# Two more places for expert weights, other waits ahead of their loads, and a part of the state chain moved, in two transformer blocks with 32 experts

## The reference

```python
h = h + mixed @ w_out[l]                       # mixed = [retention, recurrence]
xn = rms_norm_2(h, norm2_gain)
# each token goes to 2 of 32 experts, D = 1024, D_EXPERT = 512
def expert_block(args):
    xblk, e = args
    hdn = jax.nn.silu(xblk @ w_gate[e]) * (xblk @ w_up[e])
    return hdn @ w_down[e]
# recurrence, step by step
sa = einsum('bhvk,bhk->bhv', state, a_t)
state = state * w_t + sa[..., None] * b_t + v_t[..., None] * k_t
```

## Time and profile before

| | us |
|---|---|
| timed runs | 1047.58, 1049.62, 1049.64 |
| median | 1049.62 |
| the profiled execution, its own time | 1047.48 |
| its span (first to last instruction) | 1045.7 |
| TensorE busy | 900.0 |
| VectorE busy | 436.9 |
| ScalarE busy | 318.1 |

### The profile page before, as it was taken

How to read it: one execution, slowest core, us unless ns; L and a number is a source line. 1 busy time by engine, 2 the same in 40 slices (tenths; PEclk the granted TensorE clock), 3 DMA queues, 4 the chain that set the end, 5 groups by cost and what they waited for, 6 DMA issues and landing times.

```text
span 1045.7 us, 17915 instructions
## 1 busy us (share of the span) xinstructions
PE 900.0 (86%) x7768; PEld 642.5 (61%) x7768; DVE 436.9 (42%) x553; ACT 318.1 (30%) x410; POOL 17.5 (2%) x34
## 2 busy tenths in 40 slices
PE   5999999999999998999999997776868677677854
PEld 5999988999999878999988732221313122121311
DVE  4577777666656437996676510000101010010101
ACT  4457674554444327644443400000000000000002
POOL 1300000000000000000000000000000000000000
PEclk9999999999999999999999999998989888998999
DMA  9994334555654544353019999999999999999994
GB/s 338 269 325 147 133 111 162 161 162 171 204 190 161 201 155 163 129 205 115 3 56 387 420 398 422 422 421 420 421 421 423 421 422 422 421 422 423 422 421 193
DMA packets 84439, 294.97 MB, mean 282 GB/s; under 512 B 5903, under 2 KB 35231, under 8 KB 59664
## 3 DMA queue, kind: packets, MB, share of 16 engines
q1 hardware_dynamic: 79280, 284.18, 69.8%
q10 hardware_dynamic: 3552, 6.08, 1.6%
q0 software_dynamic: 1536, 3.68, 1.3%
HBM read 290.77 MB, written 4.10 MB: 282 GB/s over the span
## 4 chain that ended last, share of the span: by engine, by line
PE 55%; DMA 31%; SPq 5%; DVE 5%; issue 2%; ACT 1%; DVEq 0%; ACTq 0%
PE psum L986 13%; DMA arena<-in_w_down 13%; PE psum L987 13%; PE psum L988 13%; DMA arena<-in_w_up 12%; DMA arena<-in_w_gate 5%; SPq L837 5%; PE psum L1572 4%; PE psum L1315 3%; PE psum L961 2%; PE psum L1592 2%; DVE ring_rounded L2055 1%; PE psum L953 1%; PE psum L1061 1%; DVE arena L2103 1%
## 5 line engine op out<-in xcount | busy, mean ns | idle before, releaser
L1572 PE MATMUL psum<-arena,featL 128*32 128x512 f32 x1024 | 172.1, 657 | 63.6 <-DMA arena<-in_w_up 48.6
L2055 DVE TENSOR_TENSOR ring_rounded<-arena,hi_rounded 128x2048 fp32r<-128x2048 f32 x77 | 176.0, 2290 | 94.7 <-ACT hi_rounded L1677 93.8
L1677 ACT ACTIVATE hi_rounded<-arena 128x2048 fp32r<-128x2048 f32 x77 | 146.7, 1912 | 157.5 <-PE psum L988 52.4
L986 PE MATMUL psum<-hi_rounded,featT_rounded 128*128 128x256 f32 (+1 forms) x560 | 165.2, 295 | 4.7 <-DVE featL_rounded L2071 3.9
L987 PE MATMUL psum<-ring_rounded,featT_rounded 128*128 128x256 f32 (+1 forms) x560 | 162.6, 290 | 0.0
L988 PE MATMUL psum<-hi_rounded,featL_rounded 128*128 128x256 f32 (+1 forms) x560 | 162.5, 290 | 0.0
L1572 PEld LDWEIGHTS psum<-arena,featL 128*32 128x32 f32 x1024 | 38.7, 118 | 184.9 <-DMA arena<-in_w_up 86.3
L1592 PE MATMUL psum<-arena,featT 128*32 128x512 f32 x488 | 91.7, 673 | 40.9 <-DMA arena<-in_w_down 36.0
L986 PEld LDWEIGHTS psum<-hi_rounded,featT_rounded 128*128 128x128 f32 x560 | 108.0, 193 | 8.3 <-DVE ring_rounded L2055 4.2
L987 PEld LDWEIGHTS psum<-ring_rounded,featT_rounded 128*128 128x128 f32 x560 | 108.1, 193 | 1.2
L988 PEld LDWEIGHTS psum<-hi_rounded,featL_rounded 128*128 128x128 f32 x560 | 108.0, 193 | 1.3
(11 more groups left out here) (295 smaller groups left out, 1138.9 us busy)
## 6 DMA issues: line engine op xcount, KB each, us to landing
arena<-in_w_gate SPq DMA_DIRECT2D x75, 1024.0 KB, 26.2
arena<-in_w_up SPq DMA_DIRECT2D x75, 1024.0 KB, 26.4
arena<-in_w_down SPq DMA_DIRECT2D x62, 1024.0 KB, 26.9
arena<-in_w_in SPq DMA_DIRECT2D x14, 2048.0 KB, 8.9
arena<-in_w_down SPq DMA_DIRECT2D x5, 2048.0 KB, 7.7
arena<-in_w_out SPq DMA_DIRECT2D x3, 2048.0 KB, 8.6
arena<-in_w_in SPq DMA_DIRECT2D x4, 1024.0 KB, 9.6
t_copies<-arena ACTq DMA_DIRECT2D x1, 2048.0 KB, 8.0
```

What stands on the lines that cost most here:

```text
L986: mm(o, lhs[0], rhs[0], start=start, stop=False, skip_group_check=True)
L1572: ins = mm(psum[32 * j:32 * j + 32, MB[4 + m], :], xg[:, 4 * half + k, 32 * j:32 * j + 32], quad[place(q, j)][j][:, 512 * k:512 * k + 512] ...
L1677: fn(high, view, ACT.Copy).then_inc(hi_ready, 1)
L2055: tt(low, view, high.bitcast(F32), ALU.subtract).then_inc(lo_ready, 1)
```

## The change

- **Places.** `SPLIT` adds a place 6 for j = 2 (half in `featL`, half in `featT`, where the space of the one-hot rows is laid out anew) and for j = 3 (1024 floats in `rows`, where the final gain goes later, 512 in `featT`, 512 in a new tile `late`). `ONCE` becomes (2, 1, 2, 2), and `FIRST` lists for each j in which place its first loads go. A split piece comes in two or three DMAs. `held` finds its columns.
- **Waits.** `place_free` names a place and the pieces in it; the waits ahead are others, and in another order. To make this possible the mask `mle` moves out of the stretch of `cst` that a piece overwrites, the inverse's P2T to another slot, and the states S from `arena` into free halves of `xn`.
- **Final gain.** GpSimd loads it behind its four small products and behind eight read pieces.
- **Chain.** The keys of state 0 go ahead of WT on TensorE. `root` goes ahead of the copies of Q and gn on ScalarE, and `ret_scale(1)` ahead of TT on VectorE.

The diff, cut to its core:

```diff
-LE = layout(("G", 256), ("Gw", 256), ("GT", 256), ("sg", 512), ("h", 512))
+LE = layout(("G", 256), ("Gw", 256), ("sg", 512), ("h", 512), ("GT", 256), ("gap", 256))
...
-             ("reset", T), ("gap2", 64), ("wina", 64),
-             ("mAdT", 64), ("mAd", 64), ("m16T", 64), ("m32T", 64), ("mlt", 64), ("mle", 64), ("id64", 64),
+             ("mle", 64), ("reset", T), ("gap2", 64), ("wina", 64),
+             ("mAdT", 64), ("mAd", 64), ("m16T", 64), ("m32T", 64), ("mlt", 64), ("id64", 64),
...
-        AdT, Ad, o16T, o32T, X, P2, P2T = (piece(M0 + 1024 * n, NT, 8, CH) for n in (0, 1, 2, 3, 12, 13, 4))
+        AdT, Ad, o16T, o32T, X, P2, P2T = (piece(M0 + 1024 * n, NT, 8, CH) for n in (0, 1, 2, 3, 12, 13, 11))
...
-        S = piece(LM["RT"][0], NCH, 4, 64)
+        S = [xn[:, c // 2, 512 + 256 * (c % 2):768 + 256 * (c % 2)].rearrange("p (i v) -> p i v", v=64) for c in range(NCH)]
...
+        late = sb("late", [P, 512])
+        SPLIT = {2: (featL[:, 4:8, :].rearrange("p a b -> p (a b)"), spent[:, LE["sg"][0]:LE["h"][1]]),
+                 3: (final_gain, spent[:, LE["GT"][0]:LE["gap"][1]], late[:])}
...
-        ONCE = (2, 1, 1, 1)
+        ONCE = (2, 1, 2, 2)
+        FIRST = [(*PLACES, NQ, NQ + 1)] * 2 + [(PLACES[0], NQ + 2, *PLACES[1:], NQ)] * 2
...
-                    at = quad_place(r, pair, q, j)
-                    nc.sync.dma_start(quad[at][j], w[:, j, 2048 * half:2048 * half + 2048]).then_inc(quad_in[at][j], 16)
+                    at, lo = quad_place(r, pair, q, j), 2048 * half
+                    for part in (quad[at][j],) if at < NQ + 2 else SPLIT[j]:
+                        nc.sync.dma_start(part, w[:, j, lo:lo + part.shape[1]]).then_inc(quad_in[at][j], 16)
+                        lo += part.shape[1]
...
+                    wait_filled(sp, "ro", NT - 1)
+                    place_free(2, 0, 1)
+                    wait_filled(sp, "mat", "Arb", 1)
+                    place_free(3, 3)
+                    sp.wait_ge(mixed_ready, 1)
+                    place_free(2, 2)
+                    wait_filled(sp, "gn", NT - 1)
+                    place_free(NQ, 0, 1)
+                    wait_filled(sp, "mat", "Ark", 1)
+                    place_free(3, 2)
                     sp.wait_ge(mixed_ready, NT)
-                    load_quad(0, 0, 0, pieces=(1, 2, 3))
-                    wait_emptied(sp, "mat", "Ark", 1)
-                    load_quad(0, 0, NQ, pieces=(0, 1))
-                    for key, pieces in RELEASED:
-                        wait_filled(sp, *key)
-                        for q, k in pieces:
-                            load_quad(0, 0, q, pieces=(k,))
+                    wait_filled(sp, "U", NCH - 1, 1)
+                    place_free(2, 3)
+                    wait_filled(sp, "Y", 1, 1)
+                    place_free(3, 0, 1)
                     sp.wait_ge(mixed_ready, 2 * NT)
-                    load_quad(0, 0, NQ, pieces=(2,))
-                    load_quad(0, 0, 2, pieces=(2,))
+                    place_free(NQ, 2)
+                    place_free(1, 2)
                     wait_filled(sp, "wo2", 0, 1)
-                    load_quad(0, 0, 2, pieces=range(2))
-                    load_quad(0, 0, 3, pieces=(3,))
+                    place_free(1, 0, 1)
+                    place_free(0, 3)
                     wait_filled(sp, "wo2", 1, 0)
-                    load_quad(0, 0, 2, pieces=(3,))
-                    load_quad(0, 0, 3, pieces=(0,))
+                    place_free(1, 3)
+                    place_free(0, 0)
                     wait_filled(sp, "wo2", 1, 1)
-                    load_quad(0, 0, 3, pieces=(1, 2))
+                    place_free(NQ + 2, 2, 3)
+                    place_free(0, 1, 2)
...
-            wait_filled(pool, "logit", NT - 1)
-            nc.gpsimd.dma_start(final_gain, A["final_gain"].to_broadcast([P, D])).then_inc(gain_in, 16)
...
+            pool.wait_ge(pieces_read, 8)
+            nc.gpsimd.dma_start(final_gain, A["final_gain"].to_broadcast([P, D])).then_inc(gain_in, 16)
...
+            st0 = state_keys(0)
             banks = [begin("WT", c).rearrange("p (t i q) -> p t i q", t=NT, i=4) for c in range(2)]
...
-            st0 = state_keys(0)
             u_inner(0)
...
                 if name == "Z2":
                     high_moved("mT", 0, 0)
+                    root(48, RET_H, RET_D, 1)
...
-                    root(48, RET_H, RET_D, 1)
...
                 if name == "Z2":
                     low_moved("mT", 0, 0)
-                if name == "TT":
                     ret_scale(1)
```

## The result

The changed kernel is slower, by less than half a per cent. Its median is 1050.78 us (1048.24 to 1059.39, 19 runs) against 1047.59 (1045.03 to 1052.51, 19 runs) for the kernel before, 3.2 us more. Forecast were 3.3 us less.

The account below looks back on a forecast made before the run. The prediction took the unbroken expert-weight DMA stream (about 421.7 GB/s) as the bound. Queue -3.5, split pieces +0.4 and chain -0.2 gave -3.3 us, from the median 1049.62 to 1046.3; range 1042.5 to 1049.8.

Parts of the forecast that it names:

- the model of the queue's holes: Expert-weight queue: 23 places close the 601 to 605 hole, unbroken run from 576.5, end at 1025.3, 3.5 us less.
- The final gain: Its 0.52 MB load moves from ahead of the idle hole into the unbroken run, costing 1.25 us.
- the moved steps: TensorE chain up to 574.38: keys of state 0 ahead of WT gain 0.2 us; the moved scaling and root, zero.
- the split pieces: Two pieces in DMAs with 4 and 2 KB rows, 2.1 MB in all: taken as 0.4 us more.
- The bound from above: For the split pieces: 2.1 MB at w_out_2's 376 GB/s instead of 422, 0.6 us more.
- The estimate of 1.2: For the split pieces: at the skill's 341 GB/s for a single 1 MB DMA, 1.2 us lost.
- rival 2: Expert traffic in 499.6 to 504.6 and 533.7 to 545.8 delays TensorE's instruction fetches; slower 0.06, most gain eaten 0.14.
- The price of one fetch: In rival 2: 1.0 us per delayed fetch; slower only with five or six delays, or fewer longer ones.
- The argument against it: Against rival 2: in 545 to 555 DMA already ran at 379 GB/s with TensorE busy 9.2 of 10 us.
- what the early loads bring: Ahead of the unbroken run: each MiB landed before it is worth 2.49 us.
- Rival 3: Early places come late in SyncE's order, so only the added places count: 1.6 us gained, 1048.0; chance 0.14.
- Rival 1: Full gain or more: the 557.2 stall shrinks by 1.0 us, splitting is free, -4.7, 1044.9; 0.66 together with the forecast.

Follow-up runs that it names:

- late_no_split: late_all without the two added places: 21 places, no piece in parts, the final gain's load where the change puts it; 1050.43 us, ratio 1.0021.
- chain_only: The kernel before with only the three moved chain steps, its first expert loads also waiting for U of chunk 0; 1047.84 us, ratio 1.0005.
- rows_4k: The kernel before with the two pieces issued at 586.84 us cut into four DMAs with rows of 4 KB; 1047.65 us, ratio 0.9997.
- late_all: The changed kernel with its six early pieces issued only when TensorE has U of chunk 0; 1047.0 us, ratio 0.9992.
- late_parts: The changed kernel, its six early pieces and piece 3's `late` part waiting for U of chunk 0, its `rows` part for VectorE's last U copy; 1043.81 us, 0.9967.
- old_chain: The changed kernel with the keys of state 0, the square root and the scaling back in their old order; 1049.83 us, ratio 1.0021.
- traffic_at_ro: The kernel before with four unused 1 MiB copies, all issued when the retention output is filled (near 497 us); ratio 1.0046.
- traffic_on_before: The kernel before with four unused 1 MiB copies, issued at Arb, the first scaled retention half and gn; 1056.83 us, ratio 1.0085.

## Why the prediction was wrong, point by point

**Right: the model of the queue's holes.** 23 places close the hole of 601 to 605 (416 GB/s), the queue is empty just before 577 (183 GB/s in 574 to 577; it was forecast empty up to 576.5, and the sum of wo2 came 1.6 us later than in before), and the last stretch runs at 421. The start-up time, too, fits. The final gain was rightly taken from the idle hole into the bill: 1.25 us forecast, and late_no_split shows 1.8 in all.

**Right: the moved steps cost nothing.** chain_only, 1.0005. VectorE's last step, of two instructions, stood at 539.89 and 540.82 in before and was forecast there; it came at 537.81 and 538.79, which counted from the `ro` copy is 0.2 us later, behind TensorE's pause of 0.30 us for the first late fetch. In chain_only it is 0.7 us or more earlier than in before. The 0.2 us gained can't be seen at this resolution.

**Wrong in size: the split pieces.** Taken at 0.4 us, with bounds 0 and 0.6, from the rate of w_out_2. The row length was costed rightly (0.3 us in rows_4k). What failed is the assumption that a piece in parts differs from a whole one in nothing but its rows: 587 to 600 at 370 instead of 419 GB/s is 1.5 us, and the unequal end of the DMA engines is 0.8. Together 2.3 in place of 0.4, which leaves 1.2 of the 3.5 us that the queue should have gained; 0.8 were measured, and 0.4 isn't placed. The bound from above was the error: a nearest row with shorter rows in an unloaded queue is no bound for five DMAs into four tiles in a full one. The estimate of 1.2 that I worked out from the Trainium skill ("DMA: Bandwidth & Descriptors", section Bandwidth) was nearer than my bound, though its reason, the size of one DMA, isn't what the runs show: rows_4k has DMAs of 512 KB at 408 to 412 GB/s.

**Wrong: the step that decided, the price of the early traffic.** The prediction has this mechanism as its rival 2, a fetch of TensorE's instructions that expert traffic holds back, and gives "slower" 0.06. Three steps of it failed.
1. The price of one fetch. I took the difference of two stalls, 1.0 us, and asked for five or six of them. Two fetches in a row under a queue at 348 to 418 GB/s, 3.3 and 6.2 us late, cost a stall of 3.05 us. Priced one by one, a second late fetch behind the first wasn't in the rival's sum.
2. The argument against it. "545 to 555 has DMA at 379 GB/s too and TensorE busy 9.2 of 10 us" is true and proves little. The one fetch of TensorE's that starts in that stretch, at 550.63, is 3.1 us late; TensorE went on, so it must have had instructions left. The next, at 556.86, is 3.4 us late, and that is the stall of 2.05 us at 557.2. A busy TensorE was no sign of a fetch in time.
3. The consequence. A stall under which TensorE is idle isn't paid once: the granted clock was 0.50 for the next 10 us. Against late_all the chain lost 4.0 us. The stall is 3.05 of it; the half clock on the work behind it should be the rest (by difference; no run has the one without the other), and the stall of 1.77 us at 556.7 of late_all, which after doesn't have, gives some of it back.

**Wrong: what the early loads bring.** I counted each early MiB as 2.49 us. But up to 577 the places that are free are few, and the queue catches up. In after it stands idle in 546 to 552 (3 GB/s) and again in 574 to 577; late_all uses this very time for the pieces that it has not loaded early. Its window ahead of the sum of wo2:

```profile
565.00:570.00 5.00, 5.00 (x42) 4.82 (x41) 1.70 (x4) 1.20 (x2) 0.00 (x0) 1.00 1.01 419
```

By 574 to 577 it, too, falls to 341 GB/s: it has caught up. With the six pieces issued together behind 543 the queue takes 456.3 us, with them early 456.0. The prediction's own sum had this in it: its twelve pieces landed by 573.6 "and the queue is empty for 2.9 us". The slack of the queue ahead of 574 had to be set against the early loads, and it would have shown that they could be left out. What brings the gain is the number of places and what fills them, which late_parts gets without early traffic.

**Rival 3** (late places, 1048.0) is, by late_all, nearly that: 1047.0, ratio 0.9992, and harmless. **Rival 1**'s step came true, the stall at 557 is gone in after, where DMA is idle, but at the price of a larger one.

**What stays open.** Why the stretch with parts into `featL`, `featT`, `rows` and `late` runs at 317 to 348 GB/s for 7 to 10 us in five kernels and at 391 in late_parts; why a fetch in a loaded queue starts some 3 us late; and 0.4 us of the queue.

## What to carry to other kernels

Free DMA time beside a dense run of small TensorE instructions isn't free: the instructions themselves come by DMA, fetches that come late one behind the other stop the engine, and the clock can fall behind the stop. Before loads are moved earlier, ask whether the queue runs dry again before the point that sets the end; if it does, early loads gain nothing and only the number of places counts. Use idle queue time for the awkward transfers (in parts, short rows) in place of the ones that would be fast anyway, and put them where TensorE can bear it.

## What the runs showed of the hardware that I had not expected

- A fetch of TensorE's instructions under a loaded queue: TensorE stood still for 3.05 us (after), 2.78 (old_chain), 2.87 (traffic_at_ro), where stalls with idle DMA were 0.5 to 1.1.
- With a loaded queue a fetch started 2.9 to 3.5 us after the record at which it starts when DMA is idle (the first ones of the table, before's among them), and the second one between the inverse's steps 6.1 to 7.3 us (after, old_chain, traffic_on_before).
- With such stops the granted clock was 0.50 (1.2 GHz) for 10 us in after, 7 in old_chain and traffic_at_ro, about 14 in traffic_on_before. Behind the stop of 2.05 us in before it stayed at 1.00.
- 4 MiB of traffic that touches nothing cost 8.7 us, at another place 4.8, with rows of 2 KB 5.6; 1 MiB cost 1.0 us (between nothing and 2.6).
- Pieces cut into parts near 590 us cost something 440 us later: the DMA engines ended the last expert load further apart, 0.8 to 1.0 us.
- At one and the same point of the program, the stretch with parts of pieces moved at 317 to 348 GB/s in some kernels and at 391 in another, and 4 KB rows into plain places at 412.
